# Moving three of four rotary rotation groups of retention heads 1 to 3 from VectorE to GpSimd, and head 0's rotation into the first three branch blocks

## What is computed

```python
def rotary(t):
    ...
    t1, t2 = tf[..., : d // 2], tf[..., d // 2:]
    out = jnp.concatenate([t1 * cos - t2 * sin, t1 * sin + t2 * cos], axis=-1)
...
        qb = rotary(split_heads(r_q, RET_HEADS))
        kb = rotary(split_heads(r_k, RET_HEADS)) * (RET_KEY_DIM ** -0.5)
        vb = split_heads(r_v, RET_HEADS)
        ret = chunkwise_retention(qb, kb, vb)
        ret = rms_norm(ret, ret_out_gain[layer][None, :, None, :])
        out_b = merge_heads(ret) * jax.nn.silu(r_g)
        p_a = jnp.einsum('bsw,wd->bsd', out_a, w_branch_sb[layer])
        p_b = jnp.einsum('bsw,wd->bsd', out_b, w_branch_ret[layer])
```

## Time and profile before

| what | value |
|---|---|
| median of 3 runs | 3002.91 us (2995.93 to 3012.65) |
| the profiled execution | 3008.91 us |
| its span in the profile | 3007.0 us |
| mean granted clock of TensorE | 0.957 of full speed |
| TensorE busy | 2810.8 us, 93% |
| VectorE busy | 1383.8 us, 46% |
| ScalarE busy | 960.9 us, 32% |
| GpSimd busy | 140.2 us, 5% |

### The profile page before, as it was taken

The page is one execution under the profiler, slowest core; times in us unless marked ns, Lnnn a source line. Parts: engine busy times, 40 slices in busy tenths (PEclk is TensorE's granted clock), DMA queues, the critical chain, the costliest instruction groups (busy, mean ns, idle before and its releaser), DMA issues.

```text
span 3007.0 us, 35931 instructions
## 1 busy us (share of the span) xinstructions
PE 2810.8 (93%) x14762; PEld 2311.8 (77%) x14762; DVE 1383.8 (46%) x1818; ACT 960.9 (32%) x1567; POOL 140.2 (5%) x231
## 2 busy tenths in 40 slices
PE   5999999998889999987699999998999999999998
PEld 4778888886667778545598677876798998979888
DVE  7565555555556543564324481366324223232232
ACT  6453222336556551112113241233314112021122
POOL 0111111110000001000010000000010000000000
PEclk7999999999999999999899999896799999999999
DMA  2322333240121124321133001000021111111112
GB/s 93 105 89 95 110 110 109 99 162 24 67 84 52 49 74 158 136 91 42 56 111 112 28 1 40 32 29 0 32 88 43 43 57 43 43 57 43 43 49 86
DMA packets 128553, 209.25 MB, mean 70 GB/s; under 512 B 6013, under 2 KB 106538, under 8 KB 124826
## 3 DMA queue, kind: packets, MB, share of 16 engines
q1 hardware_dynamic: 109610, 144.79, 14.3%
q0 software_dynamic: 18800, 62.38, 5.8%
HBM read 161.02 MB, written 46.14 MB: 69 GB/s over the span
## 4 chain that ended last, share of the span: by engine, by line
PE 83%; DVE 7%; ACT 4%; issue 2%; DVEq 1%; DMA 1%; ACTq 1%; SPq 0%; POOL 0%
PE ps L428 22%; PE ps L1854 19%; PE ps L422 19%; PE ps L1951 4%; PE ps L1935 2%; PE ps L2194 2%; PE ps L1910 2%; PE ps L2261 1%; PE ps L2276 1%; PE ps L2007 1%; PE ps L1995 1%; PE ps L2074 1%; PE ps L1921 1%; PE ps L1864 1%; PE ps L2324 1%
## 5 line engine op out<-in xcount | busy, mean ns | idle before, releaser
L407 DVE TENSOR_TENSOR w_lo<-w_raw,w_hi 128x2048 fp32r<-128x2048 f32 x60 | 137.5, 2292 | 410.2 <-ACT w_hi L403 410.2
L403 ACT ACTIVATE w_hi<-w_raw 128x2048 fp32r<-128x2048 f32 x60 | 114.8, 1913 | 591.0 <-DMA w_raw<-in_w_ff 363.6
L428 PE MATMUL ps<-a_hi,w_hi 128*128 128x512 f32 x736 | 294.7, 400 | 4.6 <-issue 3.3
L428 PE MATMUL ps<-a_lo,w_hi 128*128 128x512 f32 x736 | 292.3, 397 | 0.0
L428 PE MATMUL ps<-a_hi,w_lo 128*128 128x512 f32 x736 | 290.2, 394 | 0.0
L422 PE MATMUL ps<-w_lo,f_hi 128*128 128x256 f32 x1024 | 289.8, 283 | 0.0
L422 PE MATMUL ps<-w_hi,f_hi 128*128 128x256 f32 x1024 | 289.8, 283 | 0.0
L422 PE MATMUL ps<-w_hi,f_lo 128*128 128x256 f32 x1024 | 289.8, 283 | 0.0
L1367 DVE TENSOR_TENSOR proj_out<-ps,proj_out 128x512 f32<-128x512 f32 x210 | 141.8, 688 | 240.1 <-PE ps L1854 240.1
L1854 PE MATMUL ps<-t_hi,pw_hi 128*128 128x512 f32 x480 | 196.4, 409 | 4.0 <-DVE t_lo L1341 4.0
L422 PEld LDWEIGHTS ps<-w_hi,f_hi 128*128 128x128 f32 x1024 | 196.6, 192 | 0.2
(11 more groups left out here) (342 smaller groups left out, 5773.0 us busy)
## 6 DMA issues: line engine op xcount, KB each, us to landing
w_raw<-in_w_ff SPq DMA_DIRECT2D x32, 1024.0 KB, 5.4
pw_raw<-in_w_in SPq DMA_DIRECT2D x30, 1024.0 KB, 5.5
projections<-proj_out POOLq DMA_DIRECT2D x88, 256.0 KB, 3.3
w_raw<-in_w_in SPq DMA_DIRECT2D x20, 1024.0 KB, 5.2
projections<-proj_sq POOLq DMA_DIRECT2D x32, 256.0 KB, 2.7
w_raw<-in_w_out SPq DMA_DIRECT2D x8, 1024.0 KB, 5.2
x_in<-in_x SPq DMA_DIRECT2D x8, 512.0 KB, 5.4
q<-projections SPq DMA_DIRECT2D x4, 1024.0 KB, 4.9
```

The costliest lines, as they stand in the source:

```text
L403: act.activation(W_hi[s][:, :, :], W_raw[s][:, :, :], ACT.Copy).then_inc(w_hi, 1)
L407: dve.tensor_tensor(W_lo[s][:, :, :], W_raw[s][:, :, :], W_hi[s][:, :, :].bitcast(f32), ALU.subtract).then_inc(w_lo, 1)
L428: last = pe.matmul(bank[banks[j]][:, :], w[s][:, k, ct * P:(ct + 1) * P], a[:, k, t0 + th * HALF:t0 + (th + 1) * HALF], start=(k == 0 and ...
```

## The change

`rotate` becomes a helper that takes the engine and the semaphore. For heads 1 to 3, group 0 stays on VectorE behind step 0 of the head before, and groups 1, 2 and 3 go to GpSimd, which has four scratch tiles of its own (`RTP`, tile `rtp`), in memory that is free in this stage. They stand in GpSimd's stream between the first branch's gate loads and its wait for the last norm. TensorE waits before scores(h, 0) for 4 + h signals of VectorE and 3h of GpSimd. For head 0 all groups stay on VectorE, but groups 0 and 1 come behind the first branch block, 2 behind the second, 3 behind the third, and none behind the fourth.

```diff
@@ -149,6 +149,7 @@
     RK = [at("rk0", [P, 2, SEQ], off=a_at + 8 * KB), at("rk1", [P, 2, SEQ], off=work_at + 8 * KB)]
     rcos = at("rcos", [P, SEQ], off=a_at + 16 * KB)
     rsin = at("rsin", [P, SEQ], off=a_at + 20 * KB)
+    RTP = [at(f"rtp{u}", [P, HALF], off=work_at + (16 + 2 * u) * KB) for u in range(4)]
     RT = [at(f"rt{u}", [P, HALF], off=a_at + (24 + 2 * u) * KB) for u in range(4)]
     RV = [at("rv0", [P, TT, BC], off=out_at + 24 * KB), at("rv1", [P, TT, BC], off=work_at + 24 * KB)]
     decay = [at(f"decay{h}", [P, SEQ], off=o) for h, o in enumerate((out_at + 16 * KB, work_at + 64 * KB, work_at + 40 * KB))]
@@ -467,7 +468,7 @@
         pa_stored = [sem(f"pa_stored{u}") for u in range(2)]
         stage_free = sem("gate_staging_free")
         mg_in, mg_sig = [sem(f"merge_gate{j}_in") for j in range(4)], sem("merge_gate_sigmoid")
-        rot_ok = sem("rotated")
+        rot_ok, rot_pool = sem("rotated"), sem("rotated_by_pool")
         rqk_in, rvd_in = [sem(f"rqk{s}_in") for s in range(2)], [sem(f"rv_and_decay{s}_in") for s in range(2)]
         rg_in = [sem(f"rg{s}_in") for s in range(2)]
         a_done, at_ready, rv_part = sem("scores_done"), sem("decayed_ready"), sem("retained_part_done")
@@ -570,6 +571,20 @@
                 eng.wait_ge(post_done, 32 + turns_before(before[-1]) + j + 1)
             elif before:
                 eng.wait_ge(c_stored[out_tile(n, j)], stores_before(n, j))
+
+        def rotate(eng, h, m, signal):
+            s, src, th, tmp = h % 2, (RQ, RK)[m // 2], m % 2, RTP if h and m else RT
+            eng.wait_ge(rqk_in[s], 32 * (h // 2) + 32)
+            c, sn = rcos[:, th * HALF:(th + 1) * HALF], rsin[:, th * HALF:(th + 1) * HALF]
+            t1, t2 = src[s][:, 0, th * HALF:(th + 1) * HALF], src[s][:, 1, th * HALF:(th + 1) * HALF]
+            eng.tensor_tensor(tmp[0][:, :], t1, c, ALU.mult)
+            eng.tensor_tensor(tmp[1][:, :], t2, sn, ALU.mult)
+            eng.tensor_tensor(tmp[2][:, :], t1, sn, ALU.mult)
+            eng.tensor_tensor(tmp[3][:, :], t2, c, ALU.mult)
+            eng.drain()
+            eng.tensor_tensor(t1, tmp[0][:, :], tmp[1][:, :], ALU.subtract)
+            eng.tensor_tensor(t2, tmp[2][:, :], tmp[3][:, :], ALU.add).then_inc(signal, 1)
+            eng.drain()
 
         @block.sync
         def _(sp):
@@ -753,6 +768,10 @@
                     gate_again(ms_d, 2 * b + 2, j)
             for u in range(2):
                 pool.wait_ge(pa_stored[u], 16 * 12)
+            pool.wait_ge(const_in, 16 * (3 + len(spec)))
+            for h in range(1, 4):
+                for m in range(1, 4):
+                    rotate(pool, h, m, rot_pool)
             pool.wait_ge(ret_scaled, 16)
             for b in range(4):
                 for j in range(4):
@@ -1486,20 +1505,6 @@
             split_lo(dve, B1, 0)
             split_lo(dve, B1 + 1, 1)
 
-            def rotate(h, m):
-                s, src, th = h % 2, (RQ, RK)[m // 2], m % 2
-                dve.wait_ge(rqk_in[s], 32 * (h // 2) + 32)
-                c, sn = rcos[:, th * HALF:(th + 1) * HALF], rsin[:, th * HALF:(th + 1) * HALF]
-                t1, t2 = src[s][:, 0, th * HALF:(th + 1) * HALF], src[s][:, 1, th * HALF:(th + 1) * HALF]
-                dve.tensor_tensor(RT[0][:, :], t1, c, ALU.mult)
-                dve.tensor_tensor(RT[1][:, :], t2, sn, ALU.mult)
-                dve.tensor_tensor(RT[2][:, :], t1, sn, ALU.mult)
-                dve.tensor_tensor(RT[3][:, :], t2, c, ALU.mult)
-                dve.drain()
-                dve.tensor_tensor(t1, RT[0][:, :], RT[1][:, :], ALU.subtract)
-                dve.tensor_tensor(t2, RT[2][:, :], RT[3][:, :], ALU.add).then_inc(rot_ok, 1)
-                dve.drain()
-
             dve.wait_ge(const_in, 16 * (3 + len(spec)))
             for i in range(4):
                 n = B1 + i
@@ -1510,7 +1515,8 @@
                     dve.tensor_tensor(PA[:, 2 * i + ct, META + th * HALF:META + (th + 1) * HALF], bank[j], NB[j][:, :], ALU.mult).then_inc(kept[j], 1)
                 if i < 2:
                     split_lo(dve, n + 2, i)
-                rotate(0, i)
+                for m in ((0, 1), (2,), (3,), ())[i]:
+                    rotate(dve, 0, m, rot_ok)
 
             def head_norm(h):
                 for j in range(4):
@@ -1534,8 +1540,8 @@
                     if kb >= 2 or h:
                         dve.wait_ge(rv_part, 8 * h + kb - 1)
                     dve.tensor_tensor(AT[kb % 2][:, 0:w], wide(4 + 2 * (kb % 2), w), decay[h][:, 0:w], ALU.mult).then_inc(at_ready, 1)
-                    if kb < 4 and h < 3:
-                        rotate(h + 1, kb)
+                    if kb == 0 and h < 3:
+                        rotate(dve, h + 1, 0, rot_ok)
                     if kb == 5 and h:
                         head_norm(h - 1)
                 if h < 2:
@@ -1986,7 +1992,9 @@
                 if kb >= 2 or h:
                     pe.wait_ge(at_ready, 8 * h + kb - 1)
                 if kb == 0:
-                    pe.wait_ge(rot_ok, 4 * h + 4)
+                    pe.wait_ge(rot_ok, 4 + h)
+                    if h:
+                        pe.wait_ge(rot_pool, 3 * h)
                     if h >= 2:
                         pe.wait_ge(rn.rs, 2 * h - 2)
                 for lo in range(0, w, HALF):
```

## The result

The changed kernel takes 3020.52 us (median of 20 runs, 3010.84 to 3029.42) against 3002.85 us (20 runs of the kernel before beside them): ratio 1.005, 95% interval 1.0036 to 1.0064. It is slower by half a per cent, some 15 us. The forecast of 3024 us had the direction and the size; how the sum is made up is another matter.

The account below looks back on a forecast made before the run. TensorE, busy 93% of the span, was taken as the bound. Turns between VectorE and GpSimd added 5.2, 7.9 and 8.2 us in heads 0 to 2, +21.3 on 3002.9: 3024 us, range 2994 to 3050.

Parts of the forecast that it names:

- Head 0 starts at once: Start of head 0: with no rotation behind block four, TensorE's 4.55 us gap and 2.2 us of slow clock go.
- The landing does not move, at(1) is queued behind it: Head 0, step 1: head 1's keys still land at 1231.7, so 2.8 of 6.75 us won are waited away.
- Two-sided interference, in turns: Behind each key landing: VectorE and GpSimd rotations alternate in reading SBUF; chance 0.48, 3024 us.
- What the turns cost a group: VectorE's group beside GpSimd: six operations each wait 1.15 us, 6.9 us added, 10.85 in all.
- head 0's +3.0 at step 1: Head 0: at(1) ends at 1243.6 against a weigh at 1240.68; with 2.2 us of clock +5.2.
- Head 1's 6.3 us of waiting: Head 1, step 1: at(1) 6.9 us later makes TensorE wait 6.3 us; with clock, less 0.63, +7.9.
- The clock: TensorE falls to its lower clock after the long wait in each of heads 0, 1 and 2: 2.2 us each.
- GpSimd is hidden: Start of head 1: GpSimd needs 25.6 us a head, TensorE wants it 32.7 us after the landing, so no wait.
- The signs named ahead: Prompt head 0, VectorE operations of some 1.8 us, waits of 6 to 10 us, clock 0.50, none for GpSimd.
- Rival A: No interference: VectorE keeps its pace beside GpSimd, -5.4 us, 2997 us; chance 0.20.
- B: Interference in part: VectorE waits half a GpSimd operation, 3.45 us a group, +7 to +11, 3012 us; chance 0.18.
- C: GpSimd slow, or blocking VectorE for more than one operation: at 2.0 us an operation +40, 3043 us; chance 0.12.

Follow-up runs that it names:

- e1: Changed kernel with only head 0's new placement kept, all rotations of heads 1 to 3 back on VectorE: 0.9993 of the kernel before, stage 153.2 us.
- e3: Changed kernel with each of GpSimd's 54 rotation operations replaced by a 128x512 memset that reads nothing: 0.9987 of the kernel before, stage 153.2 us.
- e8: Changed kernel with GpSimd rotating one group of each later head instead of three, VectorE the rest: 1.008 of the kernel before, stage 167.3 us.
- e4: Changed kernel plus one 128x1 subtraction and a drain on GpSimd ahead of its first rotation: 1.0049 of the kernel before, stage 177.0 us.
- e2: Changed kernel with head 0's rotation placed as before, only the GpSimd part kept: 1.0069 of the kernel before, stage 173.9 us.
- e10: The changed kernel unaltered, run once more for a second profile: stage 171.1 us, one run.
- e7: Changed kernel plus a drain alone on GpSimd ahead of its first rotation: stage 171.1 us, one run.

## Why the prediction was right, and where it was not

- **Head 0 starts at once: right.** The 4.55 us and the slow scores went; the second group behind block 1 cost nothing: TensorE has no idle time in the first branch blocks.
- **The landing does not move, at(1) is queued behind it: right in head 0.** Keys landed at 1232.8, 10.3 us after the last evacuation began (10.2 predicted); e1 measured the 2.8 us by itself as 2.85. I had not charged the clock for it; e1 shows that it falls (1.8 us).
- **Two-sided interference, in turns: right**, by e3 (goes with reads) and e8 (goes with the six turns, not with the work).
- **What the turns cost a group: mis-sized.** The sum had + 6 x 1.15 = 6.9 us a head, 10.85 for the rotation. Measured are 8.06, 10.26 and 9.21 us (first rotation operation to at(1)): a turn adds 1.07 us, and the first operation, or the last, often goes free. So head 0's +3.0 at step 1 was +0.3 (19.47 us after the mark instead of 19.18).
- **When the group starts, against TensorE: left out.** Head 1's 6.3 us of waiting was 3.62, head 2's 7.6 was 4.45; the turns explain 0.6 and 1.6 us of that. The sum kept the start of VectorE's group fixed against weigh(h,0), TensorE's first matmuls with the values. It moved, since TensorE itself came later. In head 1 the group began 0.3 us behind weigh(1,0) before (1265.95 and 1265.67). In the changed kernel it began 1.6 ahead of it (1272.15 and 1273.76), since TensorE had waited for GpSimd and the keys had landed meanwhile. In head 2 the group began 1.7 us behind before and 0.3 in the changed kernel, where the clock had fallen behind step 6 of head 1 and made TensorE 1.4 later, but not the keys. The wait in head 2 follows this distance: 4.45 us at 0.3 behind, 7.01 and 7.07 at 2.9 behind (e4, e2), 2.88 at 1.3 ahead (e10). VectorE's group in head 1, before and in the changed kernel:

```profile
1265.95 0.69 DVE L1494 TENSOR_TENSOR rt<-rq,rcos 128x512 f32<-128x512 f32 x1 [1.80 <-DMA rk<-projections]
```

```profile
1272.15 1.74 DVE L580 TENSOR_TENSOR rt<-rq,rcos 128x512 f32<-128x512 f32 x1
```

- **The clock: right in kind.** Predicted 2.2 us behind each of three waits; measured 1.6, 3.0 and 1.8 (first weigh against 3.17), and 1.7 more behind a fourth.
- **"GpSimd is hidden": failed.** This step said 25.6 us a head. It took 32.6 us (1232.92 to 1265.5): 18 operations at 1.23 instead of 1.15, 5.6 us for the first drain where the sum had 0.15, and 2.0 us for a collision with the low part of a weight block, less the turns, which delayed it by 1.8 us and not 4.0. And TensorE, which had lost less at step 1, asked for head 1 at 1262.3, 29.3 us after the landing and not 32.7. It waited 3.4 us for it in head 1, and the clock took 1.7. The errors cancel, so that the nearness of 3024 to 3020.5 is in part luck: head by head +7.1, +7.3 and +2.6 us against +5.2, +7.9 and +8.2. Part of head 2's small number is the clock: the fall at step 6 that head 2 has in the earlier trace rows was in head 1 in the changed kernel, 1.4 us each way.
- The stage grew by 16.9 us, the medians by 17.7; the profiled span by 13.2, since the stage began 1.0 us later and what follows it was 4.7 us shorter in that one execution.
- **The signs named ahead.** Head 0's start, operations of some 1.8 us (1.75) and the clock at 0.50 came. Waits of 6 to 10 us for at(1) in every head came in head 0 alone, and "no wait for GpSimd's rotations" was wrong in the first profile and right in the second.
- Rival A is out by the 1.75 us operations. B (half an operation, + 3.45 us a group) is out in its beat, but a group lost 4.1, 6.2 and 5.2 us, which is between B and the full 6.9. C is out in its form (a GpSimd operation alone took 1.26, not 1.6 or more) but not in its symptom, the wait at a head's start.

## What to carry to other kernels

Work that is moved to GpSimd to relieve VectorE did not run beside it here where both read two SBUF operands: look at what else the same landing releases, and count a turn for every VectorE operation that somebody waits for. Before moving work to another engine, look at what is queued behind a wait on the first: here head 0's rotation earlier, one step's delay of a group, the norm two steps later and one wait moved in SP's queue gave 16.6 us of stage with no engine added. And when one wait goes, look for the next: here it stood in SP's queue, which waited for the norm that had been moved. A wait also depends on how late the waiting engine is itself, so waits of successive heads do not simply add up.

## What was not expected of the hardware

- GpSimd's first drain behind its first operations of this stage took 5.54 to 5.57 us in e2, e3, e8 and both profiles of the changed kernel; one drain ahead of time removes it (e4, e7). Later ones show 0.16 us of idle time, sometimes 0.46.
- A two-input 128x512 fp32 operation takes GpSimd 1.26 us (1.23 from start to start); the estimate from the Trainium skill's figure for 2048 columns (GPSIMD Engine Reference, section 3.1), a quarter of it, was 1.12. A 128x512 memset takes 0.52.
- Waits of about 3 us lower TensorE's clock in some places (2.85 us in e1) and not in others: behind the waits of 2.98 us in the kernel before, heads 1 and 3 kept it (1.57 us for the eight matmuls behind it) and head 2 did not (2.93 us). What decides it, no run here settles.
